# mLSTM heads of a pair taken together, by halves of the tokens, on alternating row groups of TensorE

## Chip, core and metric

The kernel runs on one core of one Trainium2 chip. The metric is the device time of one launch in microseconds. It is compared as the median of several runs.

## What is computed

Two blocks of a hybrid network run one after the other on 1024 tokens with a model width of 1024. The change touches only one of the three mixers of the second block, the mLSTM. The reference for it, cut to the core (chunks of `CHUNK` tokens, 4 heads, 64 key and 128 value channels):

```python
def mlstm_memory(q, k, v, i_pre, f_pre):
    log_f = jax.nn.log_sigmoid(f_pre)
    qc, kc, vc = (_to_chunks(a) for a in (q, k * dk ** -0.5, v))
    ...
    def step(carry, inp):
        mem, norm, m_prev = carry
        qi, ki, vi, ii, lfi = inp
        b = jnp.cumsum(lfi, axis=-1)
        a_inter = b + m_prev[..., None]
        d_intra = jnp.where(causal, b[..., :, None] - b[..., None, :] + ii[..., None, :], -jnp.inf)
        m_t = jnp.maximum(a_inter, jnp.max(d_intra, axis=-1))
        w_inter = jnp.exp(a_inter - m_t)
        scores = jnp.einsum('bhtd,bhsd->bhts', qi, ki) * jnp.exp(d_intra - m_t[..., None])
        num = (w_inter[..., None] * jnp.einsum('bhtd,bhdv->bhtv', qi, mem)
               + jnp.einsum('bhts,bhsv->bhtv', scores, vi))
        den = w_inter * jnp.einsum('bhtd,bhd->bht', qi, norm) + jnp.sum(scores, axis=-1)
        h = num / jnp.maximum(jnp.abs(den), jnp.exp(-m_t))[..., None]
        ...
```

Around it stand the large products (a 1024 x 1024 activation with weights), which make up most of the kernel's work.

## The kernel before

**Layout.** Channels lie on the 128 partitions and the 1024 tokens along the free axis. Every large product is made of three matmuls per block of 128 channels: each weight is split by GpSimd into a high and a low part (`WH`, `WL`; `split_tile`, L541 to L544) and each activation too (`UH`, `UL`). A weight tile takes 48 matmuls of 512 columns on TensorE. `PG` (4 banks of PSUM) holds the results of two tiles in turns; `PX` (the other 4 banks) is for everything else.

**Fill.** While TensorE would wait for VectorE or ScalarE inside a mixer, it works on weight tiles of later products: `fill(n)` from `next_units` (L715) issues n quarters of a tile, 12 matmuls each. The rest of a stage's tiles is issued by `product` (L666).

**The mLSTM** runs in the PE program from L912 on, for two pairs of heads (`b` = 0, 1). The two heads of a pair (`hh` = 0, 1) share tiles: their queries and keys lie on partitions 0 to 63 and 64 to 127 of `WK[:, 2]`, `WK[:, 3]` and `WK[:, 8]` (queries times decay). Tokens are taken in 8 tiles of 128. For each pair: decay rows are spread over partitions (L935), values and weighted keys are transposed (L947), the state of each tile is made (L956, then VectorE L2484 and L2487). After that come the heads, one after the other, each over all 8 tiles, with this order on TensorE:

- spread: for each half of the tokens, a matmul of 4 partitions spreads the head's row over 128 partitions of bank 0 or 1 (L968), and a matmul with the mask is added to it (L970); `fill(1)`
- scores: 8 matmuls of 64 partitions, keys with queries, into banks 2 and 3 (L975); `fill(2)`
- numerators: wait for `m["p"]`, then for each half 4 matmuls of the 128 x 128 scores with values (L985, 129 columns, the last one the row sum), and the matmuls of 64 partitions of queries with the state added to them (L989, none for tile 0); a `fill(1)` stands between the halves; then `fill(2)`
- wait for `m["h"]`, 8 transposes (L995) into banks 2 and 3, `fill(2)`

ScalarE makes the exponentials of the spread rows (L1604) after it has taken two finished tiles out of `PG` (`gate_out`, L1521). VectorE multiplies them by the scores (L2494, `m["p"]`), makes the denominators from the last column of each numerator (L2504 to L2512), divides (L2515, `m["h"]`), and multiplies the transposed result by the output gate (L2521, `m["y"]`). The next head's spread waits for `m["y"]`. SyncE waits for `m["y"]` before it loads into `WK[:, 6]` for the S5 mixer that follows (L445), and GpSimd before its phasors (L552).

Of the kernel before, what the change touches and what calls it, by code (L numbers as in the profile page):

```python
# [12 lines left out]
ALU = mybir.AluOpType  # L13
# [3 lines left out]
P = 128  # L17
# [9 lines left out]
TT = T // P  # L27
# [65 lines left out]
def program(nc, dram, out):  # L93
# [168 lines left out]

    def S5P(k):

        return WK[:, 14, 16 * k:16 * k + 16]
# [88 lines left out]
    with block:  # L354

        @block.sync
        def _(sp):
# [81 lines left out]
            def s5_load(i):  # L439

                sp.wait_ge(s5["staged"], 16 * i + 16)
                if i:
                    sp.wait_ge(s5["y"], i)
                else:
                    sp.wait_ge(m["y"], 3)  # L445
# [160 lines left out]
        def _(pe):  # L606
# [310 lines left out]
            for b in range(2):  # L917
# [43 lines left out]
                for hh in range(2):  # L961
                    head = 2 * b + hh
                    rows = slice(64 * hh, 64 * hh + 64)
                    if hh:
                        pe.wait_ge(m["y"], head)

                    for half in range(2):
                        pe.matmul(PX[:, half, :], SEL[0:4, P * head:P * head + P],  # L968
                                  WK[0:4, 13, 512 * half:512 * half + 512], start=True, stop=False)
                        mm = pe.matmul(PX[:, half, :].rearrange("p (t c) -> p t c", c=P), IDENT_R[:],  # L970
# [3 lines left out]
                    for t in range(TT):  # L974
                        mm = pe.matmul(PX[:, 2 + t // 4, P * (t % 4):P * (t % 4) + P],  # L975
                                       WK[rows, 3, P * t:P * t + P], WK[rows, 2, P * t:P * t + P],
                                       start=True, stop=True)
                    mm.then_inc(m["scores"], 1)
                    fill(2)
                    pe.wait_ge(m["p"], head + 1)  # L980
                    for half in range(2):
                        if half:
                            fill(1)
                        for t in range(4 * half, 4 * half + 4):
                            pe.matmul(ml_bank(0, t), WK[:, 11, P * t:P * t + P], ml_v(hh)[:, VW * t:VW * t + VW],  # L985
                                      start=t % 3 == 0, stop=False)
                        for t in range(4 * half, 4 * half + 4):
                            if t:
                                mm = pe.matmul(ml_bank(0, t), WK[rows, 8, P * t:P * t + P], ml_state(t)[rows],  # L989
                                               start=False, stop=t in (2, 5, 7))  # L990
                    mm.then_inc(m["num"], 1)
                    fill(2)
                    pe.wait_ge(m["h"], head + 1)
# [1913 lines left out]
```

## Time and profile before

| | us |
|---|---|
| median of 3 runs | 2278.82 |
| lowest and highest | 2274.89, 2280.83 |
| the profiled execution | 2281.79 |
| its span | 2280.0 |
| TensorE busy in it | 2233.6 |

All times of rows come from the profiled execution. In a timeline the first number is the start and the second the time to the end of the last instruction of the row. Matmuls are pipelined, so what a matmul costs TensorE is the distance from its start to the start of what follows. A float32 matmul stands as two records in the trace, one of a split (`fp32r`) operand as one.

### The profile page before, as it was taken

What the parts mean: (1) busy time and instruction counts of PE and PEld (TensorE: products, weight loads), DVE (VectorE), ACT (ScalarE), POOL (GpSimd) and SP (SyncE); (2) the same over time, 40 slices, a digit from 0 to 9 for tenths busy, and PEclk for the clock granted to TensorE, in tenths of its full rate; (3) what the DMA queues carried; (4) which work ended last, traced back from release to release, by engine and by line L of the source; (5) the groups of instructions that cost most, each with busy time, mean ns of one, the idle gap of its engine ahead of it and who ended that gap; (6) DMA issues with size and microseconds to landing.
All of it is one profiled execution on the core that took longest, in us unless ns stands there. A gap on an engine that the chain in (4) does not pass through costs nothing.

```text
span 2280.0 us, 29813 instructions
## 1 busy us (share of the span) xinstructions
PE 2233.6 (98%) x11328; PEld 1812.9 (80%) x11328; DVE 1061.2 (47%) x1203; ACT 618.2 (27%) x722; POOL 1160.6 (51%) x1114
## 2 busy tenths in 40 slices
PE   7999999999999999999999999999999999999997
PEld 5788887787778787787878888777888888888886
DVE  7888873357623251351596246455432101223406
ACT  6553342335433231121133232243211000111112
POOL 3332224666643232232684344565666776666776
PEclk9999999999999999999999999999999999999999
DMA  6224422232421111111333344424323333323343
GB/s 226 80 103 179 169 84 91 87 101 90 141 83 37 56 56 47 56 56 56 93 120 120 107 143 138 157 92 157 101 92 101 102 101 101 101 92 101 111 166 120
DMA packets 79385, 240.36 MB, mean 105 GB/s; under 512 B 7728, under 2 KB 19136, under 8 KB 79296
## 3 DMA queue, kind: packets, MB, share of 16 engines
q1 hardware_dynamic: 66944, 220.25, 28.8%
q10 hardware_dynamic: 12352, 18.88, 2.2%
q8 instruction: 62, 1.02, 0.2%
q14 instruction: 27, 0.22, 0.0%
HBM read 209.73 MB, written 29.36 MB: 105 GB/s over the span
## 4 chain that ended last, share of the span: by engine, by line
PE 84%; issue 4%; POOL 3%; DVE 3%; ACT 2%; POOLq 2%; DMA 1%; DVEq 1%; SPq 1%; ACTq 0%
PE PG L625 38%; PE PG L666 17%; PE PG L715 15%; PE PG L1086 5%; POOL WL L544 2%; POOLq L543 1%; DMA WRAW<-up_w 1%; PE PX L820 1%; PE PX L744 1%; PE PX L815 1%; DVE WK L1840 1%; PE PX L835 1%; DVEq L2772 1%; PE PX L798 0%; DVE XR L2773 0%
## 5 line engine op out<-in xcount | busy, mean ns | idle before, releaser
L544 POOL TENSOR_TENSOR WL<-WRAW,WH 128x1024 fp32r<-128x1024 f32 (+2 forms) x304 | 708.9, 2332 | 45.1 <-issue 0.9
L541 POOL TENSOR_TENSOR TOUCH<-TOUCH 128x2 f32<-128x2 f32 x304 | 81.6, 268 | 1048.5 <-PE PG L715 349.6
L625 PE MATMUL PG<-UL,WH 128*128 128x512 f32 x1072 | 418.8, 391 | 0.0
L625 PE MATMUL PG<-UH,WH 128*128 128x512 f32 x960 | 377.7, 393 | 5.2 <-POOL WL L544 3.7
L625 PE MATMUL PG<-UH,WL 128*128 128x512 f32 x960 | 374.6, 390 | 0.0
L542 POOL TENSOR_SCALAR WH<-WRAW 128x1024 fp32r<-128x1024 f32 (+2 forms) x304 | 311.4, 1024 | 0.0
L625 PEld LDWEIGHTS PG<-UL,WH 128*128 128x128 f32 x1072 | 202.4, 189 | 43.5 <-issue 1.7
L666 PE MATMUL PG<-UH,WH 128*128 128x512 f32 x576 | 226.4, 393 | 3.1 <-DVE WK L1950 1.6
L715 PE MATMUL PG<-UH,WH 128*128 128x512 f32 x544 | 223.7, 411 | 2.4 <-POOL WL L544 2.4
L666 PE MATMUL PG<-UH,WL 128*128 128x512 f32 x576 | 224.2, 389 | 0.0
L666 PE MATMUL PG<-UL,WH 128*128 128x512 f32 x576 | 224.1, 389 | 0.0
L625 PEld LDWEIGHTS PG<-UH,WH 128*128 128x128 f32 x960 | 180.8, 188 | 48.3 <-issue 5.7
L715 PE MATMUL PG<-UH,WL 128*128 128x512 f32 x544 | 214.4, 394 | 0.0
L715 PE MATMUL PG<-UL,WH 128*128 128x512 f32 x544 | 214.2, 394 | 0.0
L625 PEld LDWEIGHTS PG<-UH,WL 128*128 128x128 f32 x960 | 180.9, 188 | 37.8
L2708 DVE TENSOR_TENSOR WK<-WK,PG 128x512 f32<-128x512 f32 x44 | 30.3, 688 | 376.0 <-PE PG L625 367.9
L2711 DVE TENSOR_TENSOR HL<-WK,HH 128x512 f32 (+1 forms) x44 | 115.0, 2615 | 44.3 <-ACT HH L1747 44.3
L666 PEld LDWEIGHTS PG<-UH,WH 128*128 128x128 f32 x576 | 108.1, 188 | 27.8 <-issue 2.4
L625 PE MATMUL PG<-HH,WH 128*128 128x512 f32 x330 | 129.1, 391 | 0.4 <-POOL WL L544 0.4
L625 PE MATMUL PG<-HH,WL 128*128 128x512 f32 x330 | 128.4, 389 | 0.0
L625 PE MATMUL PG<-HL,WH 128*128 128x512 f32 x330 | 128.4, 389 | 0.0
L715 PEld LDWEIGHTS PG<-UH,WH 128*128 128x128 f32 x544 | 103.2, 190 | 31.1 <-issue 8.2
(504 smaller groups left out, 3522.3 us busy)
## 6 DMA issues: line engine op xcount, KB each, us to landing
WRAW<-up_w SPq DMA_DIRECT2D x88, 512.0 KB, 3.6
ADA<-ada_w SPq DMA_DIRECT2D x24, 1024.0 KB, 5.8
WRAW<-down_w SPq DMA_DIRECT2D x48, 512.0 KB, 3.7
WRAW<-out_w SPq DMA_DIRECT2D x30, 512.0 KB, 3.6
WRAW<-zg_w SPq DMA_DIRECT2D x24, 512.0 KB, 3.7
gates<-STG ACTq DMA_DIRECT2D x24, 512.0 KB, 2.6
WK<-gates SPq DMA_DIRECT2D x24, 512.0 KB, 3.4
WRAW<-gla_w SPq DMA_DIRECT2D x18, 512.0 KB, 3.7
```

The lines of the kernel that those rows point to most:

```text
L541: pool.tensor_tensor(TOUCH[:, 0:2], TOUCH[:, 2:4], TOUCH[:, 4:6], ALU.add)
L542: pool.tensor_scalar(WH[:, r, 0:n], WRAW[:, r, 0:n], 1.0, 0.0, ALU.mult, ALU.add)
L543: pool.drain()
L544: pool.tensor_tensor(WL[:, r, 0:n], WRAW[:, r, 0:n], WH[:, r, 0:n].bitcast(F32), ALU.subtract).then_inc(w_split, 1)
L625: mm = pe.matmul(PG[:, bank, :], w[:, r, P * k:P * k + P], v, start=first and k == 0 and n == 0, stop=last and k == kbs - 1 and n == 2)
L666: mm = pe.matmul(PG[:, 2 * s + half, :], w[:, r, P * k:P * k + P], x[:, k, tok], start=first and k == 0 and n == 0, stop=last and k == kbs ...
L715: mm = pe.matmul(PG[:, 2 * r + half, :], w[:, r, P * k:P * k + P], x[:, k, tok], start=k == 0 and m_ == 0, stop=k == KB - 1 and m_ == 2)
L744: mm = pe.matmul(PX[:, 2 * g + half, :], WK[:, 15, P * g:P * g + P], x_conv(i)[:, 512 * half:512 * half + 512], start=True, stop=True)
L815: pe.matmul(PX[:, half, P * (t % 4):P * (t % 4) + P], WK[:, vt[hh], P * t:P * t + P], WK[:, att[hh], P * t:P * t + P], start=t % 4 == 0, s ...
L1086: mm = pe.matmul(PG[:, 2 * r + half, :], w[:, r, P * k:P * k + P], x[k][:, tok], start=k == 0 and m_ == 0, stop=k == 3 and m_ == 2)
L2708: dve.tensor_tensor(t_, g, PG[:, 2 * n + 1, :], ALU.mult).then_inc(slot_free[n], 1)
L2711: dve.tensor_tensor(HL[:, ds(i * 2 + (n - 2 * i0), 1), :].rearrange("p a t -> p (a t)"), t_, HH[:, ds(i * 2 + n, 1), :].rearrange("p a t - ...
```

## The change

The loop over heads inside a pair becomes a loop over halves of the tokens (512 tokens, 4 tiles). Each turn takes both heads of the pair for its half, so that there are as many turns as before (4) with as many fill quarters (8 each).

- Spread: the two 4-partition matmuls stand one behind the other, head `hh` on partitions 96`hh` to 96`hh`+3 of `SEL` and `WK[:, 13]`, into banks 0 and 1; both mask matmuls follow. ScalarE copies rows 0 to 3 of `WK[:, 13]` to partitions 96 to 99 once, and `sel` is filled there too.
- Scores: the heads alternate, partitions 0 to 63 into bank 2 and 64 to 127 into bank 3.
- Numerators: the eight 128-partition matmuls stand together, then `fill(1)`, then the matmuls with the state, heads alternating. `ml_out` puts head 0 into banks 0 and 1, head 1 into banks 2 and 3, three tiles in the first bank and one in the second.
- VectorE and ScalarE do the same amount with other addresses. `SP` waits for the fourth `m["y"]` where it waited for the third.

```diff
--- before.py
+++ after.py
@@ -260,6 +260,10 @@
 
         return PX[:, b0 + t // 3, VW * (t % 3):VW * (t % 3) + VW]
 
+    def ml_out(n):
+
+        return PX[:, 2 * (n // 4) + n % 4 // 3, VW * (n % 4 % 3):VW * (n % 4 % 3) + VW]
+
     def S5P(k):
 
         return WK[:, 14, 16 * k:16 * k + 16]
@@ -442,7 +446,7 @@
                 if i:
                     sp.wait_ge(s5["y"], i)
                 else:
-                    sp.wait_ge(m["y"], 3)
+                    sp.wait_ge(m["y"], 4)
                 sp.dma_start(WK[:, 6, :], turn_in[T * i:T * i + T, :].rearrange("(q g) n -> q (g n)", g=8)
                              ).then_inc(s5["u_in"], 16)
 
@@ -958,42 +962,45 @@
                 mm.then_inc(m["ds"], 1)
                 fill(2)
                 pe.wait_ge(m["state"], b + 1)
-                for hh in range(2):
-                    head = 2 * b + hh
-                    rows = slice(64 * hh, 64 * hh + 64)
-                    if hh:
-                        pe.wait_ge(m["y"], head)
-
-                    for half in range(2):
-                        pe.matmul(PX[:, half, :], SEL[0:4, P * head:P * head + P],
-                                  WK[0:4, 13, 512 * half:512 * half + 512], start=True, stop=False)
-                        mm = pe.matmul(PX[:, half, :].rearrange("p (t c) -> p t c", c=P), IDENT_R[:],
+                for half in range(2):
+                    u = 2 * b + half
+                    if half:
+                        pe.wait_ge(m["y"], u)
+                    pair = [(hh, slice(64 * hh, 64 * hh + 64), slice(96 * hh, 96 * hh + 4)) for hh in range(2)]
+
+                    for hh, _, four in pair:
+                        pe.matmul(PX[:, hh, :], SEL[four, P * (2 * b + hh):P * (2 * b + hh) + P],
+                                  WK[four, 13, 512 * half:512 * half + 512], start=True, stop=False)
+                    for hh in range(2):
+                        mm = pe.matmul(PX[:, hh, :].rearrange("p (t c) -> p t c", c=P), IDENT_R[:],
                                        NEGMASK[:, None, :].to_broadcast([P, 4, P]), start=False, stop=True)
                     mm.then_inc(m["spread"], 1)
                     fill(1)
-                    for t in range(TT):
-                        mm = pe.matmul(PX[:, 2 + t // 4, P * (t % 4):P * (t % 4) + P],
-                                       WK[rows, 3, P * t:P * t + P], WK[rows, 2, P * t:P * t + P],
-                                       start=True, stop=True)
+                    for t in range(4 * half, 4 * half + 4):
+                        for hh, rows, _ in pair:
+                            mm = pe.matmul(PX[:, 2 + hh, P * (t % 4):P * (t % 4) + P],
+                                           WK[rows, 3, P * t:P * t + P], WK[rows, 2, P * t:P * t + P],
+                                           start=t % 4 == 0, stop=t % 4 == 3)
                     mm.then_inc(m["scores"], 1)
                     fill(2)
-                    pe.wait_ge(m["p"], head + 1)
-                    for half in range(2):
-                        if half:
-                            fill(1)
-                        for t in range(4 * half, 4 * half + 4):
-                            pe.matmul(ml_bank(0, t), WK[:, 11, P * t:P * t + P], ml_v(hh)[:, VW * t:VW * t + VW],
-                                      start=t % 3 == 0, stop=False)
-                        for t in range(4 * half, 4 * half + 4):
+                    pe.wait_ge(m["p"], u + 1)
+                    for n in range(TT):
+                        t = 4 * half + n % 4
+                        pe.matmul(ml_out(n), WK[:, 11, P * n:P * n + P], ml_v(n // 4)[:, VW * t:VW * t + VW],
+                                  start=n % 4 in (0, 3), stop=False)
+                    fill(1)
+                    for t in range(4 * half, 4 * half + 4):
+                        for hh, rows, _ in pair:
+                            n = 4 * hh + t % 4
                             if t:
-                                mm = pe.matmul(ml_bank(0, t), WK[rows, 8, P * t:P * t + P], ml_state(t)[rows],
-                                               start=False, stop=t in (2, 5, 7))
+                                mm = pe.matmul(ml_out(n), WK[rows, 8, P * t:P * t + P], ml_state(t)[rows],
+                                               start=False, stop=n % 4 >= 2)
                     mm.then_inc(m["num"], 1)
                     fill(2)
-                    pe.wait_ge(m["h"], head + 1)
-                    for t in range(TT):
-                        mm = pe.transpose(PX[:, 2 + t // 4, P * (t % 4):P * (t % 4) + P],
-                                          WK[:, 12, P * t:P * t + P], IDENT[:])
+                    pe.wait_ge(m["h"], u + 1)
+                    for n in range(TT):
+                        mm = pe.transpose(PX[:, 2 + n // 4, P * (n % 4):P * (n % 4) + P],
+                                          WK[:, 12, P * n:P * n + P], IDENT[:])
                     mm.then_inc(m["ht"], 1)
                     fill(2)
 
@@ -1589,20 +1596,22 @@
                 for n in range(2):
                     act.wait_ge(tile_done, t + 5 + n)
                     act.activation(WK[:, 6 + n, :], slot(n), ACT.Sigmoid).then_inc(slot_free[n], 1)
+                if not b:
+                    act.activation(WK[96:100, 13, :], WK[0:4, 13, :], ACT.Copy)
                 for n in range(3):
                     act.wait_ge(m["turned"], 3 * b + n + 1)
                     turned = aux(2 * (n % 2)).rearrange("p (t c) -> p t c", c=P)
                     dst = ml_v(n).rearrange("p (t c) -> p t c", c=VW)[:, :, 0:P] if n < 2 else WK[:, 9, :].rearrange(
                         "p (t c) -> p t c", c=P)
                     act.activation(dst, turned, ACT.Copy).then_inc(m["turned_copied"], 1)
-                for hh in range(2):
-                    head = 2 * b + hh
+                for half in range(2):
                     for n in range(2):
-                        gate_out(4 + 4 * b + 2 * hh + n, n, z + 2 * hh + n)
-                    act.wait_ge(m["spread"], 3 * b + hh + 2)
-                    for t in range(TT):
-                        ins = act.activation(WK[:, 11, P * t:P * t + P], PX[:, t // 4, P * (t % 4):P * (t % 4) + P],
-                                             ACT.Exp, bias=WK[:, 19, ML_AT + 4 * t + head:ML_AT + 4 * t + head + 1])
+                        gate_out(4 + 4 * b + 2 * half + n, n, z + 2 * half + n)
+                    act.wait_ge(m["spread"], 3 * b + half + 2)
+                    for n in range(TT):
+                        at = ML_AT + 4 * (4 * half + n % 4) + 2 * b + n // 4
+                        ins = act.activation(WK[:, 11, P * n:P * n + P], PX[:, n // 4, P * (n % 4):P * (n % 4) + P],
+                                             ACT.Exp, bias=WK[:, 19, at:at + 1])
                     ins.then_inc(m["e"], 1)
 
 
@@ -2487,38 +2496,36 @@
-                for hh in range(2):
-                    head = 2 * b + hh
-                    dve.wait_ge(m["e"], head + 1)
-                    dve.wait_ge(m["scores"], head + 1)
+                for half in range(2):
+                    u, tok = 2 * b + half, slice(512 * half, 512 * half + 512)
+                    dve.wait_ge(m["e"], u + 1)
+                    dve.wait_ge(m["scores"], u + 1)
                     dve.tensor_tensor(WK[:, 11, :], WK[:, 11, :], aux(2), ALU.mult).then_inc(m["p"], 1)
-                    dve.wait_ge(m["num"], head + 1)
-
-                    em = WK[:, 19, ML_AT + 32:ML_AT + 64].rearrange("p (t h) -> p t h", h=4)[:, :, head]
-                    parts = []
-                    for b0, nb, nt in ((0, 2, 3), (2, 1, 2)):
-                        num = PX[:, b0:b0 + nb, 0:nt * VW].rearrange("p b (t c) -> p b t c", c=VW)
-                        at = slice(3 * b0, 3 * b0 + nb * nt)
-                        parts.append((num, at, den[:, at].rearrange("p (b t) -> p b t", t=nt)))
-                    for num, _, d_ in parts:
-                        dve.tensor_scalar(d_, num[:, :, :, P], -1.0, None, ALU.mult)
+                    dve.wait_ge(m["num"], u + 1)
+
+                    em = WK[:, 19, ML_AT + 32:ML_AT + 64].rearrange("p (t h) -> p h t", h=4)[:, 2 * b:2 * b + 2,
+                                                                                            4 * half:4 * half + 4]
+                    den_of = den.rearrange("p (h t) -> p h t", t=4)
+                    y_of = WK[:, 12, :].rearrange("p (h t c) -> p h t c", h=2, c=P)
+                    parts = [(PX[:, b0:4:2, 0:VW * (t1 - t0)].rearrange("p h (t c) -> p h t c", c=VW), slice(t0, t1))
+                             for b0, t0, t1 in ((0, 0, 3), (1, 3, 4))]
+                    for num, at in parts:
+                        dve.tensor_scalar(den_of[:, :, at], num[:, :, :, P], -1.0, None, ALU.mult)
...
-                    for num, at, d_ in parts:
-                        ins = dve.tensor_tensor(
-                            WK[:, 12, P * at.start:P * at.stop].rearrange("p (b t c) -> p b t c", c=P, t=d_.shape[2]),
-                            num[:, :, :, 0:P], d_[:, :, :, None].to_broadcast([P, d_.shape[1], d_.shape[2], P]),
-                            ALU.mult)
+                    for num, at in parts:
+                        ins = dve.tensor_tensor(y_of[:, :, at], num[:, :, :, 0:P],
+                                                den_of[:, :, at, None].to_broadcast([P, 2, at.stop - at.start, P]), ALU.mult)
                     ins.then_inc(m["h"], 1)
-                    dve.wait_ge(m["ht"], head + 1)
-                    dve.tensor_tensor(H[:, 4 + head, :], aux(2), WK[:, 6 + hh, :], ALU.mult).then_inc(m["y"], 1)
+                    dve.wait_ge(m["ht"], u + 1)
+                    dve.tensor_tensor(H[:, 4 + 2 * b:6 + 2 * b, tok], PX[:, 2:4, :], WK[:, 6:8, tok], ALU.mult
+                                      ).then_inc(m["y"], 1)
 
 
             def half(s_, h):
@@ -2855,7 +2862,7 @@
     if_b[32:36], if_b[64:68] = f["ml_i_b_2"][0], f["ml_f_b_2"][0]
     sel = np.zeros((P, 6 * P), np.float32)
     for h in range(4):
-        sel[h, P * h:P * (h + 1)] = 1.0
+        sel[[h, 96 + h], P * h:P * (h + 1)] = 1.0
         for r in (32, 64):
             sel[r + h, 4 * P + 64 * h:4 * P + 64 * (h + 1)] = 1.0
```

## Rows read from the trace of the kernel before

**Rows 1.** The profile's page, part 1: busy time, share and instructions of each engine.

```profile
PE 2233.6 (98%) x11328; PEld 1812.9 (80%) x11328; DVE 1061.2 (47%) x1203; ACT 618.2 (27%) x722; POOL 1160.6 (51%) x1114
```

**Rows 2.** What TensorE waited for from 840 to 1100 us, the two longest of three.

```profile
PE PG L666 <- ACT WK L1582: 0.8, 1, 0.8
PE PX L947 <- ACT WK L1597: 0.5, 2, 0.2
```

**Rows 3.** The chain of work in order of time: start, us, what.

```profile
859.62 1.99 PE PX L935 x8
...
926.86 4.33 PE PG L715 x12
...
1034.11 2.74 PE PG L715 x12
```

**Rows 4.** TensorE's timeline, first head of the second pair: start us, us, instruction.

```profile
1031.08 1.12 PE L968 MATMUL PX<-WK 4*128 4x512 f32 x2
1032.13 0.50 PE L970 MATMUL PX<-NEGMASK,IDENT_R 128*128 128x512 f32 x1
1032.56 1.12 PE L968 MATMUL PX<-WK 4*128 4x512 f32 x2
1033.61 0.50 PE L970 MATMUL PX<-NEGMASK,IDENT_R 128*128 128x512 f32 x1
1033.95 0.39 PE L715 MATMUL PG<-UH,WH 128*128 128x512 f32 x1
...
1036.78 2.05 PE L975 MATMUL PX<-WK 64*128 64x128 f32 x16
1038.76 0.50 PE L715 MATMUL PG<-UH,WH 128*128 128x512 f32 x1
1039.10 0.39 PE L715 MATMUL PG<-UL,WH 128*128 128x512 f32 x1
...
1044.34 1.05 PE L985 MATMUL PX<-WK 128*128 128x129 f32 x8
1045.32 0.93 PE L989 MATMUL PX<-WK 64*128 64x129 f32 x6
1046.19 0.50 PE L715 MATMUL PG<-UH,WH 128*128 128x512 f32 x1
...
1050.02 1.16 PE L989 MATMUL PX<-WK 64*128 64x129 f32 x8
1051.11 0.50 PE L715 MATMUL PG<-UH,WH 128*128 128x512 f32 x1
...
1056.69 1.03 PE L995 MATMUL PX<-IDENT,WK 128*128 128x128 f32 x8
1057.48 0.48 PE L715 MATMUL PG<-UH,WH 128*128 128x512 f32 x1
```

**Rows 5.** TensorE's timeline in the S5 mixer, the output matmuls of one block.

```profile
1140.10 2.06 PE L1058 MATMUL PX<-WK 64*128 64x128 f32 x32
1142.08 0.50 PE L715 MATMUL PG<-UH,WH 128*128 128x512 f32 x1
```

**Rows 6.** By stretch: from:to us, length, TensorE busy (instructions), clock, DMA share, GB/s.

```profile
893.40:896.80 3.40, 3.40 (x10) 0.50 0.51 170
```

**Rows 7.** VectorE's timeline, last head: numerators done to output.

```profile
1083.25 0.23 DVE L2504 TENSOR_SCALAR WK<-PX 128x6 f32<-128x6 f32 x2 [11.06 <-PE PX L989]
...
1083.86 1.24 DVE L2509 TENSOR_TENSOR WK<-WK 128x8 f32<-128x8 f32 x1
...
1085.44 1.29 DVE L2515 TENSOR_TENSOR WK<-PX,WK 128x768 f32<-128x768 f32 x2
1089.82 1.23 DVE L2521 TENSOR_TENSOR H<-PX,WK 128x1024 f32<-128x1024 f32 x1 [3.08 <-PE PX L995]
```

**Rows 8.** ScalarE's timeline, the transposed values of the first pair.

```profile
872.52 1.94 ACT L1597 ACTIVATE WK<-PX 128x1024 f32<-128x1024 f32 x2 [13.23 <-PE PX L947]
```

**Rows 9.** SyncE's timeline: the first load of the S5 mixer's input.

```profile
1100.52 0.36 SPq L446 DMA_DIRECT2D WK<-turn_in  x1
```

More of the change, by code:

```diff
@@ L2505, in _ @@
+                    for num, at in parts:
+                        dve.tensor_scalar(den_of[:, :, at], num[:, :, :, P], -1.0, None, ALU.mult)
                     dve.drain()
-                    for num, _, d_ in parts:
-                        dve.tensor_tensor(d_, d_, num[:, :, :, P], ALU.max)
+                    for num, at in parts:
+                        dve.tensor_tensor(den_of[:, :, at], den_of[:, :, at], num[:, :, :, P], ALU.max)
                     dve.drain()
-                    dve.tensor_tensor(den, den, em,
-                                      ALU.max)
+                    dve.tensor_tensor(den_of, den_of, em, ALU.max)
@@ L2513, in _ @@
                     dve.drain()
-                    for num, at, d_ in parts:
-                        ins = dve.tensor_tensor(
-                            WK[:, 12, P * at.start:P * at.stop].rearrange("p (b t c) -> p b t c", c=P, t=d_.shape[2]),
-                            num[:, :, :, 0:P], d_[:, :, :, None].to_broadcast([P, d_.shape[1], d_.shape[2], P]),
-                            ALU.mult)
+                    for num, at in parts:
+                        ins = dve.tensor_tensor(y_of[:, :, at], num[:, :, :, 0:P],
+                                                den_of[:, :, at, None].to_broadcast([P, 2, at.stop - at.start, P]), ALU.mult)
                     ins.then_inc(m["h"], 1)
-                    dve.wait_ge(m["ht"], head + 1)
-                    dve.tensor_tensor(H[:, 4 + head, :], aux(2), WK[:, 6 + hh, :], ALU.mult).then_inc(m["y"], 1)
+                    dve.wait_ge(m["ht"], u + 1)
+                    dve.tensor_tensor(H[:, 4 + 2 * b:6 + 2 * b, tok], PX[:, 2:4, :], WK[:, 6:8, tok], ALU.mult
+                                      ).then_inc(m["y"], 1)
             def half(s_, h):
```

## Prediction

> **What bounds the kernel now.** I read the busy shares of the engines first. TensorE is busy 98% of the span, GpSimd 51%, VectorE 47% [rows 1]. That is a mean over stages, so the second view is what TensorE waited for inside the mLSTM, 840 to 1100 us. It has three waits there, 1.6 us in all, and the two longest are 0.8 and 0.5 us [rows 2]. So every microsecond that TensorE spends on the small matmuls between the fill quarters moves the end of the stage. The third view is the chain in order of time, which runs through this stage on TensorE alone, but for one short stretch on VectorE and ScalarE between the pairs, which the change leaves. The reader should look there at equal pieces with different times: 12 fill matmuls take 2.74 us at 1034.11 and 4.33 us at 926.86 [rows 3]. The fourth view is TensorE's own timeline of one head, from which the costs are taken start to start, since the recorded durations overlap [rows 4].
>
> **What one slot costs.** A float32 matmul is two records. L989 with 8 records takes 1050.02 to 1051.11, 1.09 us, and with 6 records 1045.32 to 1046.19, 0.87 us; so a record adds 0.11 us. L975 with 16 takes 1036.78 to 1038.76, 1.98 us [rows 4]. In the S5 mixer, L1058 takes the same shape (64 partitions, 128 columns) but its matmuls alternate between partitions 0 to 63 and 64 to 127 and between two banks. There 32 records take 1140.10 to 1142.08, again 1.98 us [rows 5]. Twice the work in the same time: alternating row groups run two and two. This is the pattern that the change gives to L975 and L989. For the spread matmuls the nearest row is L935: 4 partitions, 512 columns, alternating between partitions 32 and 64. It has 8 records in 1.99 us [rows 3], while two records of L968 on one row group take 1031.08 to 1032.13, 1.05 us [rows 4]. Eight of those would be over 3.8 us, so here too two run together. No row shows partitions 0 and 96 together; they are bounded by 1.05 us for the pair (full overlap, as L935) and 2.10 us (none). I take 1.05.
>
> **Spread.** Before: 1.05 for the first spread matmul, 0.43 from the mask matmul to the next spread matmul, 1.05, and 0.34 from the second mask matmul to the fill: 2.87 us [rows 4]. After: 1.05 for the pair, 0.34 for the first mask matmul (the first one behind small ones is the late one, as at 1033.61), 0.23 for the second (the 2.74 us of 12 fill matmuls divided by 12 [rows 3]): 1.62. Saved 1.25 a turn, 5.0 us in four turns.
>
> **Scores.** 16 records become 8 pairs, which by the 8-record row take 1.09 instead of 1.98 us: 0.89 a turn, 3.6 us.
>
> **Numerators.** Before, for one head: L985 to L989 0.98, L989 with 6 records 0.87, L985 0.98, L989 with 8 records 1.09, and 0.11 twice because the second fill matmul behind a change to smaller row groups comes 0.34 instead of 0.23 us after the first (1038.76 to 1039.10): 4.14 us, 8.3 for two heads [rows 4]. After: 16 records of L985 go from fill to fill. The nearest row is L995, 8 records in 0.79 us (1056.69 to 1057.48) [rows 4], plus 8 more at 0.11 and 0.09 behind them: 1.76. L989 has in the first half 12 records, 6 pairs, 0.87, in the second 16 records, 8 pairs, 1.09, each with 0.10 to enter from a fill and 0.11 to leave. The turns take 2.84 and 3.06, 5.9 in all. Saved 2.4 a pair of heads, 4.8 us for both. Half of that is overlap, half is two changes of row grouping fewer per turn.
>
> The TensorE terms are 5.0 + 3.6 + 4.8 = 13.4 us.
>
> **The clock.** From 893.40 to 896.80 TensorE was granted 0.50, its 1.2 GHz level, without having waited [rows 6]. It had just done the two spread matmuls of 4 partitions and their masks. This came behind L935 once out of two times and behind L968 twice out of four. Each time costs 4.33 - 2.74 = 1.6 us [rows 3]. The change leaves L935, but halves the time in which only 4 partitions are fed behind L968. I take both of these falls as gone, -3.2 us. The bounds are both kept (0) and, since it fell in half of the cases, two more in the turns that had none (+3.2); nothing in the new order speaks for more.
>
> **What costs nothing, and under which cover.** The ScalarE copy of 4 rows is bounded by 1.0 us, as its 1024-column activations (two take 1.94 us); ScalarE sits idle for 13.23 us before the values are transposed [rows 8], and the copy falls there. If it did not, the 0.5 us wait of L947 for ScalarE would grow by up to 1.0 us. SyncE's wait goes from the third `m["y"]` to the fourth. That is made at 1089.82 + 1.23 = 1091.05 [rows 7], and the load behind the wait goes out at 1100.52 [rows 9], 9 us later, because weight loads stand before it; the weight loads queued behind it are not held either. VectorE's steps keep their count and sizes. From the end of the numerators to `m["h"]` they take 1083.25 to 1086.73, 3.5 us [rows 7], beside 24 fill matmuls of 0.23, 5.5 us, so 2.0 us are spare; strides over banks could cost up to that for nothing. The exponentials wait for the spread and have `fill(1)`, the scores and `fill(2)` to be done; the cover shrinks by 0.9 us, from over 10 us. The transposes and the number of fill quarters per turn are unchanged, so weight tiles come due at the same points. What comes behind the mLSTM starts from its last matmuls and moves with them.
>
> **Sum.** 13.4 + 3.2 = 16.6 us. Against the profiled execution, 2281.8 - 16.6 = 2265.2. The median of the runs shown is 3.0 us below that execution. If these 3.0 are clock falls that the median run did not have, the change can't give them back, and 2265.2 stands; if they are something else, it is 2262.2. I take 2264.
>
> **Rivals.**
> - The clock falls stay, or others take their place. For it: they depend on more than the work, since the second pair of heads does the same and had none. Then 13.4 alone: 2281.8 - 13.4 = 2268.4, less part of the 3.0: 2267.
> - The pairs overlap by one step less. A matmul's two records go in order on one row group; were all records strictly in program order, only the last of one head could run beside the first of the next, and n matmuls would take n + 1 slots. That is 0.43 us more for each spread, from 4 x 0.43, and 0.11 for each of four score and four state groups: +2.6 us, 2267. L935 speaks against it: its 4 matmuls would need 5 slots, 2.1 us and what surrounds them, and took 1.99 [rows 3]. The Trainium skill, "TensorE: Matmul & The Clock Gate", Part 3, says that matmuls start and end in strict program order; read that way it gives this rival, and the trace does not agree with that reading.
> - No overlap (a bank, or partitions 0 and 96). Then only the changes of row grouping are saved: 0.8 us in the spreads and 1.7 in the numerators. 2281.8 - 2.5 = 2279.3, less part of the 3.0: 2278. If only the spread pair fails, 1.05 x 4 comes back: 2268.
> - Slower than before: each step from one head's rows to the other's is paid as a change of grouping, as from L985 to L989 or from the fill, 0.10 us [rows 4]. There are 64 records of scores, 56 of states and 16 of spreads, 136 in all; 136 x 0.10 = 13.6, less the 2.5 saved: +11, 2290. It decides from 2.5 / 136 = 0.02 us a step. L1058 with 32 such steps speaks against it [rows 5]. The Trainium skill, "TensorEngine Tiling (Array Packing)", Key Properties, says that only a change of the tiling mode drains the array, not one of the tile; L1058 agrees.
> - VectorE becomes late for the transposes. If its five small steps with new strides each took the 1.24 us of L2509 instead of 0.2 [rows 7], the chain would grow by some 5 us, 3 more than is spare, in each turn: 12 us of the gain are gone, 2277.
>
> **How the numbers follow.** Chances: forecast 0.66 (its own range 2260 to 2268), clock 0.14, one step less 0.04, no overlap 0.05 (in half of it the spread alone), slower 0.03, VectorE 0.06, something else 0.02. The range goes from 2258 (the 2262.2 and the scatter of the runs) to 2272, which takes in the clock rival, the step and the failing spread. What a measurement can tell from no change is 0.3%, 6.8 us, so faster means below 2272. Forecast, clock, step and half of no overlap are faster: 0.87. VectorE and the rest of no overlap are the same: 0.09. Slower 0.04.
>
> **What would show it.** L968 with 4 records in 1.05 us up to the mask matmuls; L975 1.1 us; L985 one group of 16; L989 with 12 and 16 records in 0.9 and 1.1 us; a clock of 1.00 behind L968; each turn some 3.4 us shorter than before at full clock. The prediction is wrong if `L995` waits for L2515 or its successor, if the distance between pairs of records is above 0.11 us, or if the stages behind 1100 us do not start earlier by what the mLSTM gained.

## The result and the profile after

| | before | changed | ratio, 95% interval |
|---|---|---|---|
| median of 5 runs each | 2275.94 | 2264.39 | 0.9936, 0.9921 to 0.9952 |
| again on another occasion: 10 and 5 runs | 2277.56 | 2260.06 | 0.9926, 0.9913 to 0.9940 |
| profiled execution | 2281.79 | 2264.55 | |
| its span | 2280.0 | 2262.8 | |

The forecast was 2264.0 in a range of 2258 to 2272. The kernel is faster by 11.6 us in the first comparison and by 17.5 us in the second; the sum of the prediction was 16.6. The profiled execution is 17.2 us shorter (2281.79 - 2264.55).

The chain of the changed kernel in order of time (start, us, what), first turn of the second pair of heads and the start of the next one. L972 is the spread, L975 its masks, L981 the scores, L989 and L996 the numerators, L1002 the transposes:

```profile
1021.62 1.06 PE PX L972 x4
...
1023.35 2.73 PE PG L719 x12
1026.08 1.09 PE PX L981 x16
1027.17 5.67 PE PG L719 x24
1032.84 1.78 PE PX L989 x16
1034.62 2.73 PE PG L719 x12
1037.36 0.87 PE PX L996 x12
1038.23 5.68 PE PG L719 x24
1043.90 0.87 PE PX L1002 x8
1044.78 5.46 PE PG L719 x24
1050.23 1.06 PE PX L972 x4
```

A turn is 1050.23 - 1021.62 = 28.6 us; a head took 32.0 before (1031.08 to 1063.11). Four records of the spread take what two took, 16 records of scores 1.09 where [rows 4] has 1.98. What TensorE waited for in the stage is as in [rows 2]:

```profile
PE PG L670 <- ACT WK L1589: 0.8, 1, 0.8
PE PX L951 <- ACT WK L1606: 0.5, 2, 0.2
```

The first pair of heads shows the clock. A stretch of 3.4 us or more in which TensorE was granted only its 1.2 GHz level (0.50) is called a fall here. The 12 fill matmuls behind the spread, which took 4.33 us in [rows 3], now take 2.73 in both turns, and the stretch of them has the full clock (from:to, length, TensorE busy, clock, DMA share, GB/s):

```profile
893.00:897.00 4.00, 4.00 (x29) 1.00 0.57 207
921.00:925.00 4.00, 4.00 (x30) 1.00 0.56 196
```

From the start of L939 (L935 before) at 859.96 to the first product behind the mLSTM at 1079.11 are 219.2 us; it was 235.6 (859.62 to 1095.26). So 16.5 us were gained there, and what comes behind took 1183.7 instead of 1184.7 us. The gain stayed.

VectorE's chain behind the numerators, which answers to [rows 7], is the one place that went another way (the last line is GpSimd's, from the same moment):

```profile
1038.28 0.23 DVE L2513 TENSOR_SCALAR WK<-PX 128x6 f32<-128x6 f32 x2 [9.77 <-PE PX L996]
1038.58 0.23 DVE L2516 TENSOR_TENSOR WK<-WK,PX 128x6 f32<-128x6 f32 x2
1038.88 2.34 DVE L2518 TENSOR_TENSOR WK<-WK 128x8 f32<-128x8 f32 x1
...
1041.57 1.29 DVE L2523 TENSOR_TENSOR WK<-PX,WK 128x768 f32<-128x768 f32 x2
...
1038.79 2.40 POOL L548 TENSOR_TENSOR WL<-WRAW,WH 128x1024 fp32r<-128x1024 f32 x1
```

The step of 8 elements (L2518, L2509 before), 1.24 us before, takes 2.34 here and 2.10 to 2.34 in the four turns. The chain is 1038.28 to 1042.86, 4.6 us instead of 3.5, and TensorE comes for the result at 1043.90.

Its new strides do not set this time. The step reads two operands from SBUF, and while it runs GpSimd is splitting a weight, an instruction of 2.40 us that reads SBUF too. The step ends when that instruction has ended: 1041.22 behind 1041.19. In the kernel before, the last head shows the same, with GpSimd further on when VectorE came (its step is the 1083.86 line of [rows 7] and ends at 1085.09, the split at 1085.07):

```profile
1082.67 2.40 POOL L544 TENSOR_TENSOR WL<-WRAW,WH 128x1024 fp32r<-128x1024 f32 x1
```

All 14 profiles have four such steps each, and all 56 end 0.02 to 0.04 us behind a GpSimd split that was running when they began. In e2 and e4 below, with the addresses of the changed kernel, the numerators come later against the split, and the step takes 2.03 and 1.57 us. What the strides alone would cost no run shows, since a split was running in every case. The steps beside it that read one operand from PSUM do not wait: the two of L2507 take 0.23 us at 1083.56, inside the same split.

### The profile page after: what moved, and what is told of

Its sections match the earlier page's. It is cut to its first block, busy times and chain, and to the rows that moved or that the text cites. A ratio compares the mean times of both kernels' runs of the same rounds, so it can differ in the third digit from the quotient of the medians.

```text
span 2262.8 us, 29814 instructions
## 1 busy us (share of the span) xinstructions
PE 2216.6 (98%) x11328; PEld 1800.7 (80%) x11328; DVE 1060.8 (47%) x1203; ACT 619.1 (27%) x723; POOL 1161.2 (51%) x1114
## 3 DMA queue, kind: packets, MB, share of 16 engines
q1 hardware_dynamic: 66944, 220.25, 28.9%
## 4 chain that ended last, share of the span: by engine, by line
PE 85%; issue 3%; POOL 3%; DVE 2%; ACT 2%; POOLq 2%; DMA 1%; DVEq 1%; SPq 0%; ACTq 0%
PE PG L629 38%; PE PG L670 17%; PE PG L719 15%; PE PG L1093 5%; POOL WL L548 2%; PE PG L732 1%; POOLq L547 1%; DMA WRAW<-up_w 1%; PE PX L824 1%; PE PX L748 1%; PE PX L819 1%; DVEq L2779 1%; DVE WK L1849 1%; PE PX L839 1%; PE PX L802 0%
## 5 line engine op out<-in xcount | busy, mean ns | idle before, releaser
L719 PE MATMUL PG<-UH,WH 128*128 128x512 f32 x544 | 223.1, 410 | 2.3 <-POOL WL L548 2.3
L719 PEld LDWEIGHTS PG<-UH,WH 128*128 128x128 f32 x544 | 102.9, 189 | 30.8 <-issue 8.5
```

Source lines behind the costliest of these rows:

```text
L719: mm = pe.matmul(PG[:, 2 * r + half, :], w[:, r, P * k:P * k + P], x[:, k, tok], start=k == 0 and m_ == 0, stop=k == KB - 1 and m_ == 2)
```

## Experiments

**Taking the alternation away, one kind at a time.** Scores (e1):

```diff
-                    for t in range(4 * half, 4 * half + 4):
-                        for hh, rows, _ in pair:
+                    for hh, rows, _ in pair:
+                        for t in range(4 * half, 4 * half + 4):
```

> The changed kernel with the score matmuls of one head behind those of the other instead of alternating; banks, counts and everything else as changed. Theory (neighbouring matmuls on partitions 0 to 63 and 64 to 127 overlap): the 16 records go from 1.09 back to 1.98 us in each of four turns, +3.6 us in the stretch of the mLSTM, nothing elsewhere. Rival (the shorter time comes from the new order of the turns, not from overlap): 1.09 us stays, +0. The span itself scatters by about as much, so the verdict is the time of the group in the timeline.

The same edit on the loop of the state matmuls (e2):

> The changed kernel with the state matmuls (queries with the state) of one head behind those of the other instead of alternating. Theory of overlap: 12 records go from 0.87 to 1.53 us and 16 records from 1.09 to 1.98 us, twice each, +3.1 us. Rival without overlap: +0. By the rival that VectorE has become late, less of the 3.1 would reach the transposes, since TensorE would wait anyway; theory: all of it.

Both heads' spread rows on partitions 0 to 3 (e3):

```diff
-                    pair = [(hh, slice(64 * hh, 64 * hh + 64), slice(96 * hh, 96 * hh + 4)) for hh in range(2)]
+                    pair = [(hh, slice(64 * hh, 64 * hh + 64), slice(0, 4)) for hh in range(2)]
```

> The changed kernel with both heads' spread matmuls on partitions 0 to 3, so on one row group. Theory of overlap: the four records take 1.9 to 2.1 us instead of 1.06, +3.4 to +4.2 us in four turns at full clock. Theory of the clock (a long stretch of 4-partition matmuls is what brings the 1.2 GHz stretches): falls behind the spread come back in some of the turns, each 1.6 us, so the median is 5 to 7 us above that of the changed kernel. Rival on the clock (the falls come by chance, whatever TensorE is fed): falls behind the spread are as rare as in the changed kernel, median 3.4 to 4.2 above.

All three edits together (e4):

> The changed kernel with all three kinds (spread, scores, states) without alternation: only the order by halves of the tokens with fewer changes of row grouping is left. Theory: of the 13.4 us of TensorE time only some 2.5 us remain, so the mLSTM stretch at full clock is 2.5 us shorter than in the kernel before and 10.9 longer than in the changed one, and the ratio to before is about 0.999. Rival (the order by halves brings the gain): the ratio stays near 0.994.

The chain of e4, first turn of the second pair, and the fill behind the second turn's spread:

```profile
1022.68 1.91 PE PX L972 x4
1025.25 2.74 PE PG L719 x12
1027.99 1.64 PE PX L981 x16
...
1039.83 1.19 PE PX L996 x12
...
1053.06 1.91 PE PX L972 x4
1055.77 4.21 PE PG L719 x12
```

The spread is as the theory of overlap says: 1.91 us for four records on one row group, 1.06 on two. So partitions 0 and 96 do overlap. The scores take 1.64 us in e1 and e4, more than 1.09 but less than the 1.98 expected, and the states 1.19 and 1.64 in e2 and e4 instead of 1.53 and 1.98. Neither theory had that. From L939 to the first product behind the mLSTM, e1 took 221.5 us and e2 221.1, so 2.3 and 1.9 more than the changed kernel, where 3.6 and 3.1 were expected. The starts of the single records in e4 tell why. Head 0 has 0, 0.21, 0.33, 0.44, 0.55, 0.66, 0.77 and 0.88 us, 0.11 apart but for the first. A further record starts at 0.555 and has the longer duration, 0.37 instead of 0.27 us, that the first record of a row group has in all these groups; seven more follow it from 0.77 on. Head 1 began when three records of head 0 were still to come. It did not wait for its turn in the program. The states of e4 show the same: the second long record starts at 0.331, ahead of those at 0.437, 0.549 and 0.66.

The medians: e3 2270.20 (6 runs, ratio 0.9948, 0.9927 to 0.9968), e4 2270.82 (11 runs, 0.9969, 0.9955 to 0.9983), with 2279.49 for before (16 runs). e3 is 5.8 us above the changed kernel's first median and 10.1 above its second, which says more of the scatter than of e3. Its profile says more: from L939 on the stage took 225.9 us, 6.7 more than in the changed kernel, about four times 0.85 for the spread and two falls of 1.6. e4 kept more than the 2.5 us forecast. Against the changed kernel it has 0.85 us more for the spread, 0.55 for the scores and 0.32 or 0.55 for the states: 1.7 us in the first turn of a pair (30.4 from 1022.68 to 1053.06, against 28.6) and 1.95 in the second, 7.3 us in four. The alternation is worth that much. The stage gained 16.5 us, 3.2 of them from the clock; so the remaining 6.0 belong to the new order, with the overlap at its borders. Measured directly, the stage of e4 took 229.9 us and that of the kernel before 235.6, 5.8 less, each with one fall behind L939 (L935 before) and two behind spreads.

**Runs of two (e9).** The scores again, with two matmuls of one head and then two of the other:

```diff
-                    for t in range(4 * half, 4 * half + 4):
-                        for hh, rows, _ in pair:
+                    for t, (hh, rows, _) in ((t, p_) for t0 in (4 * half, 4 * half + 2) for p_ in pair for t in (t0, t0 + 1)):
+                        if True:
```

> The changed kernel with the scores in runs of two matmuls per head (two of head 0, two of head 1, ...). With runs of four the 16 records took 1.64 us, between 1.09 (alternating) and 1.98 (one row group), since the first record of head 1 began while three of head 0 were still to begin. Theory (TensorE starts a matmul on an idle row group up to about three records ahead): with runs of two the second head begins one step late and then all overlap, 1.2 to 1.3 us. Rival (only neighbours overlap, the rest is in strict order): one overlapping step at each of three borders, about 1.65 us.

```profile
1025.87 1.19 PE PX L981 x16
```

1.19 us in each of the four turns. The rival of strict order (1.65) falls. The second head even began with the first, 0.014 us behind it, with three records of the first head still to come; what it lost came later. The start ahead of order is short, a few records, and enough to make strict alternation worth only 0.1 us more than runs of two.

**Changes of row grouping (e6).** The 128-partition and the 64-partition matmuls of the numerators in turns, tile by tile, behind the `fill(1)`:

```diff
-                    for n in range(TT):
-                        t = 4 * half + n % 4
-                        pe.matmul(ml_out(n), WK[:, 11, P * n:P * n + P], ml_v(n // 4)[:, VW * t:VW * t + VW],
-                                  start=n % 4 in (0, 3), stop=False)
                     fill(1)
                     for t in range(4 * half, 4 * half + 4):
                         for hh, rows, _ in pair:
                             n = 4 * hh + t % 4
+                            pe.matmul(ml_out(n), WK[:, 11, P * n:P * n + P], ml_v(n // 4)[:, VW * t:VW * t + VW],
+                                      start=n % 4 in (0, 3), stop=False)
+                        for hh, rows, _ in pair:
+                            n = 4 * hh + t % 4
                             if t:
```

> The changed kernel with the numerators by tile: two matmuls of 128 partitions (L985 of before), then the pair of 64 partitions for the same tile, and so on, so 3 and 4 stretches of 64 partitions in a turn instead of 1. Theory: each stretch of 64 partitions between matmuls of 128 costs 0.42 us beyond its slots (0.21 from its first and last step, 0.10 on the way in, 0.11 on the way out), so two and three more stretches a turn make the turns 0.8 and 1.3 us longer, +4.2 us in the mLSTM. Rival (changes of row grouping are free and the saved time in the numerators is overlap alone): +0.

```profile
1033.44 0.89 PE PX L991 x8
1034.33 0.42 PE PX L996 x4
1034.76 0.64 PE PX L991 x4
1035.40 0.42 PE PX L996 x4
...
1048.90 1.06 PE PX L972 x4
```

Four records of 128 partitions in their own company take 0.44, between groups of 64 they take 0.64; four records of 64 partitions take 0.42 where two slots are 0.22. So a stretch costs 0.4 us beyond its work. The turn from 1019.51 to 1048.90 is 29.4 us, 0.8 longer, the next one (to 1078.93) 30.0 instead of 28.9. The whole stage is 223.1 us, 3.9 more than in the changed kernel; 4.2 was expected.

**The spread pair alone in the kernel before (e5).** It spreads one head for both halves of the tokens, and puts both masks behind:

```diff
                     for half in range(2):
-                        pe.matmul(PX[:, half, :], SEL[0:4, P * head:P * head + P],
-                                  WK[0:4, 13, 512 * half:512 * half + 512], start=True, stop=False)
+                        four = slice(96 * half, 96 * half + 4)
+                        pe.matmul(PX[:, half, :], SEL[four, P * head:P * head + P],
+                                  WK[four, 13, 512 * half:512 * half + 512], start=True, stop=False)
+                    for half in range(2):
                         mm = pe.matmul(PX[:, half, :].rearrange("p (t c) -> p t c", c=P), IDENT_R[:],
...
+                if not b:
+                    act.activation(WK[96:100, 13, :], WK[0:4, 13, :], ACT.Copy)
...
-        sel[h, P * h:P * (h + 1)] = 1.0
+        sel[[h, 96 + h], P * h:P * (h + 1)] = 1.0
```

> The kernel before, in its own order (one head after the other, all tokens), with one part of the change alone: the spread matmuls of the two halves stand on partitions 0 and 96 and in front of both masks. Theory: 1.06 us for the pair and 1.24 us less a turn, so 5.0 us less at full clock; and if the long stretch of 4-partition matmuls brings the clock falls behind L968, one to two of them (1.6 us each) go as well: median 6 to 8 us below before. Rival (falls are chance): 5 us below. Rival (partitions 0 and 96 do not overlap in this order): 0 to 1 us below.

2270.38 us (6 runs), ratio 0.9971 (0.9958 to 0.9985), 7.2 us below before; a turn went from 32.0 to 30.8 us (1022.14 to 1052.92). The interval reaches from 3.4 to 9.6 us below before, so the median does not decide between 5 us and 6 to 8. The profile tells more of its own execution: from L935 to the first product behind the mLSTM it took 227.5 us, 8.2 less than in the kernel before, which is four times 1.24 and two falls of 1.6 that did not come. Its six runs lie within 2.8 us, those of before within 8.8.

**The clock behind the spread.** All profiles together tell whether chance or TensorE's work brings the falls. With the spread on one row group (before, e3, e4) 6 of 12 turns were followed by a stretch of 3.4 us at 1.2 GHz; the 12 fill matmuls behind took 4.1 to 4.3 instead of 2.73 us. With the pair (the changed kernel twice, e1, e2, e5 to e11) none of 44 turns was. So the spread on one row group brings the falls and the pair on two avoids them: in e3, the single edit that puts both on one, two falls came back. It does not bring them each time, and why it did in these six turns no run shows. An unbroken stretch isn't needed either: in the kernel before, a mask matmul of 128 partitions (0.43 us) stood between the two spread matmuls, and 2 of its 4 turns had a fall, as in e3, where they stand together for 1.91 us. Whether the shorter time at 4 partitions (1.06 us against 2.1) counts, or that two row groups work at once, is not shown.

**The other place of the kind (e7).** In the changed kernel such a fall still followed L939, in front of which stand 16 transposes of 4 by 4:

```diff
                     mm.then_inc(m["turned_rows"], 1)
+                    fill = next_units(TILE0[f"ml{b}"] + 6, UNIT0[f"ml{b}"] // 2 + 3, 6)
+                    fill(1)
                     pe.wait_ge(m["tok"], 1)
...
-                fill = next_units(TILE0[f"ml{b}"] + 6, UNIT0[f"ml{b}"] // 2 + 3, 6)
-                fill(3)
+                if b:
+                    fill = next_units(TILE0[f"ml{b}"] + 6, UNIT0[f"ml{b}"] // 2 + 3, 6)
+                fill(3 if b else 2)
```

> The changed kernel with one of the three fill quarters behind L939 moved in front of it, between the 16 transposes of 4 by 4 (1.1 us) and the 8 records of 4 partitions (2 us), for the first pair of heads only. In all profiles so far the clock fell to 1.2 GHz there. Theory (it falls after a long unbroken stretch in which few partitions are fed): the break removes that fall in most executions, -1.6 us, and the wait for VectorE of 0.3 us before L939 goes too. Rival: the fall comes all the same, -0.3 us. VectorE has the spread rows 2.7 us later, with more than 5 us to spare before the transposes of values.

```profile
858.74 1.08 PE PX L929 x16
859.82 2.96 PE PG L719 x12
862.78 1.92 PE PX L941 x8
864.70 5.68 PE PG L719 x24
```

24 fill matmuls behind it in 5.68 us: full clock. The fall was there in all 12 profiles without the edit and in none of the 2 with it (e10 is the other). From L929 to the first product behind the mLSTM it took 218.8 us, 1.7 less than in the changed kernel's first profile; 1.9 was expected. The second pair of heads is a check that needs no run: the 16 transposes stand in the first pair only, L939 with its 8 records stands in both, and in the second pair no fall came behind it in any of the 14 profiles (36 fill matmuls in 8.4 us). So L939 alone does not bring it. The median is 2258.58 (5 runs, 0.9919, 0.9904 to 0.9934), 1.5 us below the changed kernel's 2260.06 of the same occasion. The size is as expected, but the intervals overlap, so the median does not prove it.

**The gate product of GLA (e8), and both additions (e10).** Four matmuls of 16 partitions (8 records) on partitions 0 and 96:

```diff
-                        for b in range(2):
-                            for half in range(2):
-                                mm = pe.matmul(PX[:, 2 * b + half, :], A2W[:, P * b:P * b + P],
-                                               WK[0:16, 15, 512 * half:512 * half + 512], start=True, stop=True)
+                        for half in range(2):
+                            for b in range(2):
+                                rows = slice(96 * b, 96 * b + 16)
+                                mm = pe.matmul(PX[:, 2 * b + half, :], A2W[rows, P * b:P * b + P],
+                                               WK[rows, 15, 512 * half:512 * half + 512], start=True, stop=True)
...
+    misc[:, 96:112] = w2["ga"]
```

> The changed kernel with the same idea where it was not applied: the four matmuls of 16 partitions of the second gate product of GLA (8 records in 3.95 us at 606.92 in the kernel before) alternate between partitions 0 to 15 and 96 to 111; the weights of the small product that makes their input hold the 16 columns twice and the 16-row weight is loaded twice. Theory: 8 records take 2.0 us as the alternating 4-partition ones do, -1.9 us, and the 6.8 us at 1.2 GHz that follow them, which cost 3.4 us, become one of 3.4 us or none: -1.7 to -3.4 us more; median 3 to 5 us below the changed kernel. Rival (the stage is bound by the weight splits of GpSimd that wait right behind, 621 us in the chain of before): the gain is given back there, 0 to 1 us.

> The changed kernel with both additions that were run alone: the fill quarter in front of L939 and the GLA gate product on partitions 0 and 96. Theory: their gains add, 1.6 us from the clock fall behind L939 and 2.4 us around the gate product, so the median is 3 to 4 us below that of the changed kernel, 2256 to 2258, ratio to before 0.990 to 0.992. Rival (the gain of the gate product is given back in the wait for the weight splits behind it): 1.5 to 2 us below, 2258 to 2260.

The chain of e8:

```profile
606.25 1.92 PE PX L906 x8
608.17 5.69 PE PG L630 x24
...
621.04 4.16 POOL WL L549
```

The product takes 1.92 instead of 3.95 us, and no fall follows in e8 or e10. That can't be put down to the edit: of the 12 profiles without it, 7 have a fall of 6.8 us there, 3 one of 3.4 us, and e4 and e6 none (a granted clock of 1.00 from 606 to 617 us). TensorE then waits for the same weight split as in the kernel before (4.17 us at 621.35 there). Still the stage's next landmark, the first long fill of GLA, came at 639.59 instead of 646.18 in the first profile of the changed kernel and 642.04 in the second. The mLSTM (L929, L931 in e8 and e10) starts at 851.99 in e8 and 852.11 in e10; in the 12 profiles without the edit it starts between 854.04 and 859.39, the early ones being those with no fall or the short one behind the gate product. So some 2 us of the gain reach the mLSTM, and the rest of the distance to a late execution is the fall. The medians show little of it: e8 2260.10 (0.9919, 0.9904 to 0.9933), e10 2259.44 (0.9915, 0.9902 to 0.9929), e7 2258.58, the changed kernel 2260.06. None of the three is shown to beat it. For e8 3 to 5 us were expected and for e10 3 to 4, and neither came; the rival of e8, 0 to 1 us, fits its median. What e10 took from the start of the mLSTM to the end, 1406.3 us, is 2.1 more than in the first profile of the changed kernel and 0.3 less than in the second, so a single profile can't tell where its gain went. It had one fall near the end (2234 us) that neither of those two had.

**How near VectorE was (e11).** One fill quarter in front of the transposes, three behind:

```diff
                     mm.then_inc(m["num"], 1)
-                    fill(2)
+                    fill(1)
...
                     mm.then_inc(m["ht"], 1)
-                    fill(2)
+                    fill(3)
```

> The changed kernel with one fill quarter instead of two between the numerators and the transposes, and three behind them. VectorE needs 4.4 us from the numerators to L2523 in the changed kernel; one quarter is 2.7 us. Theory: TensorE waits some 1.7 us for VectorE in each turn, +6 to +7 us, and with two quarters it was 1.1 us away from waiting. Rival (what delays the transposes is not this chain): no wait, +0.

```profile
PE PX L1002 <- DVE WK L2523: 6.5, 4, 1.7
```

Four waits, 6.5 us in all, inside the 6 to 7 expected, and the stage from L939 on took 225.5 us, 6.3 more than in the changed kernel. So nothing of the wait was absorbed. With two quarters, 2.7 us more, TensorE arrives 1.0 us after VectorE is done.

**The changed kernel again (a1).**

> The changed kernel as it is, again, so that the medians below can be compared on one chip. The stretches of the mLSTM are expected as in its first profile (each turn 28.6 us from spread to spread at full clock); the median 2261 to 2265, ratio to before 0.993 to 0.994. What is open is the clock: the five first runs fell in two groups, 2259 at a mean clock of 0.996 and 2264 to 2267 at 0.994.

Its five runs lay between 2259.5 and 2262.8, with a median of 2260.06 (0.9926), a little below the range expected; its turns are 28.6 us as before. The runs of one kernel mostly order by their mean clock: the 16 of before go from 2273.2 at 0.996 to 2287.0 at 0.992. Falls also come and go where the change has no part: one at 1135 us in the changed kernel's first profile has no counterpart in that of the kernel before. This scatter can explain why two comparisons of the same two kernels gave 11.6 and 17.5 us.

## Why the prediction was right, step by step

- *Two records at a time on alternating row groups.* Right to two hundredths: spread pair 1.06 (1.05 forecast), scores 1.09, states 0.87 and 1.09, the 16 records of 128 partitions 1.78 (1.76). The turn is 3.4 us shorter, as forecast, 13.4 + 3.2 = 16.6 against 16.5 measured in the stage. The rows of another mixer (L1058) and of another product (L935) carried over because shape and order were the same.
- *The clock.* Right as to what brings and avoids the falls: the two behind L968 went, 1.6 us each, and they came back in e3 and e4. What it is worth in the median is less certain, since each execution has its own falls.
- *The profiled execution against the median.* The sum gave 2265.2, and the profiled execution of the changed kernel took 2264.55. That the first median, 2264.39, lies 0.4 us from the forecast of 2264 is in part luck: its five runs spread over 7.5 us, the second median is 2260.06, and 2264 was a choice between 2265.2 and 2262.2 that no run bears out. The sum of 16.6 us is borne out by the stage (16.5) and lies between the two comparisons of medians.
- *"No overlap" would leave 2.5 us.* Mis-sized: e4 kept 6.0 us at full clock. The step that failed is that records of one head behind those of the other share nothing; the second head starts some three records early. That gives 0.34 us in each of four score and four state groups (1.98 to 1.64, 1.53 to 1.19), 2.7 us in all. The other 0.8 is the spread: four records on one row group take 1.91 us, not twice 1.05. For the same reason the "one step less" rival is wrong in its premise, that all records start strictly in program order: strict order does not hold between row groups. The Trainium skill, "TensorE: Matmul & The Clock Gate", Part 3, states strict program order for the starts and the ends of matmuls; the starts in e4 and e9 do not agree.
- *"Half of that is overlap, half is two changes of row grouping fewer" (numerators).* 0.42 us for a stretch saved (e6) is 1.7 us in four turns, 35% of the 4.8. So the overlap gave about two thirds.
- *The slower rival.* Alternation between equal row groups costs nothing (1.09 us for 8 pairs), while a stretch of 64 partitions between matmuls of 128 costs 0.4 us, there and back (e6). This agrees with the Trainium skill, "TensorEngine Tiling (Array Packing)", Key Properties, which has a change of tiling mode drain TensorE and not a change of tile.
- *VectorE's cover.* Right that it hides the chain, wrong in the size: 1.1 us of the 2.0 us spare were used up by a single step of 8 elements. The prediction and its rival both looked to strides, and took the 1.24 us of L2509 as the price of a step. It was the time until a GpSimd split ended, and the new order of TensorE's work put the step nearer to the start of the split. The chain grew by 1.1 us instead of the rival's 5. e11 shows what it costs once the cover is gone: 1.6 us a turn.
- *ScalarE's copy and SyncE's wait at nothing.* The waits of TensorE in the stage are the same three (0.8, 0.5 and 0.3 us), and the stages behind did not get longer.

## What to carry to other kernels

Where matmuls use 64 partitions or fewer, put the independent ones on different row groups and different banks and let them follow each other; the time per pair is then that of one, and it can be read beforehand from any place of the trace that does it already. (Here the two heads always had banks of their own; what a shared bank would do, no run shows.) Put matmuls of one partition count together, since each stretch of 64 partitions between full ones cost 0.4 us beyond its work. Look at the granted clock behind matmuls of very few partitions: here the full ones behind them ran at 1.2 GHz for 3.4 us in half of the turns. Putting such matmuls on two row groups, or full ones between two groups of them, took these falls away. When a small step of VectorE takes long, look at what GpSimd was doing before blaming its addresses.

## What was not expected of the hardware

- TensorE starts a matmul on an idle row group before earlier ones of another group have begun, some three records ahead: 1.64 us in runs of four matmuls, 1.19 in runs of two, 1.09 alternating, for the same 16 records.
- The granted clock fell to 1.2 GHz though TensorE had hardly waited: not at all in front of the spreads, 0.3 us in front of L939, 0.9 us some 6 us in front of the gate product. Before the falls it had worked on spreads of 4 partitions (6 of 12 turns), on L929 and L939 (12 of 12 profiles), and on the 16-partition gate product (10 of 12 profiles).
- A VectorE step of 8 elements that reads two operands from SBUF took 1.24 us before and up to 2.34 after, since it ended only 0.02 to 0.04 us behind a GpSimd instruction that was reading SBUF when it began, in 56 of 56 cases. Steps of 2 and 6 elements with one operand in PSUM took 0.15 to 0.17 us.
